# Token shifts behind the first inverse level, and level masks by group, in a one-core RWKV-7 / S5 / attention step

## The reference

```python
z_prev = jnp.concatenate([shift_prev[:, None], za[:, :-1]], axis=1)
zs = za + p['mu'] * (z_prev - za)          # the token shift ("mix")
...
def step(S, inp):                          # for each head, each token
    r_t, w_t, k_t, v_t, kk_t, b_t = inp
    sa = jnp.einsum('bhvk,bhk->bhv', S, -kk_t)
    S = S * w_t[:, :, None, :] + sa[..., None] * b_t[:, :, None, :] + v_t[..., None] * k_t[:, :, None, :]
    return S, jnp.einsum('bhvk,bhk->bhv', S, r_t)
```

## Time and profile before

| | |
|---|---|
| median of 3 runs | 1826.49 us (1825.55 to 1827.04) |
| the profiled execution | 1829.81 us, span 1828.1 us |
| TensorE matmul busy | 1654.1 us, 90% of the span |
| VectorE busy | 725.5 us, 40% |
| GpSimd busy | 601.0 us, 33% |
| ScalarE busy | 297.5 us, 16% |
| chain that ended last | TensorE 84%, VectorE 9%, GpSimd 3%, issue 2% |

### The profile page before, as it was taken

How to read it: one execution, slowest core, us unless ns; L and a number is a source line. 1 busy time by engine, 2 the same in 40 slices (tenths; PEclk the granted TensorE clock), 3 DMA queues, 4 the chain that set the end, 5 groups by cost and what they waited for, 6 DMA issues and landing times.

```text
span 1828.1 us, 33447 instructions
## 1 busy us (share of the span) xinstructions
PE 1654.1 (90%) x14584; PEld 1578.7 (86%) x14584; DVE 725.5 (40%) x1256; ACT 297.5 (16%) x483; POOL 601.0 (33%) x356
## 2 busy tenths in 40 slices
PE   5897776888887999999999999966899999999999
PEld 5896765776776999999999999954799999999999
DVE  5655766676664442200232112857243220022100
ACT  3001223221222211100121001133122110011100
POOL 3333234333202333334333333322133333334332
PEclk9998676889897999999999999966699999999999
DMA  7541001000003344444444444330044444444442
GB/s 289 143 163 37 7 13 28 2 15 15 2 15 123 115 141 159 148 151 138 146 156 157 139 138 142 135 115 1 1 142 148 148 138 140 159 161 138 145 160 98
DMA packets 41609, 201.58 MB, mean 110 GB/s; under 512 B 13888, under 2 KB 15040, under 8 KB 19008
## 3 DMA queue, kind: packets, MB, share of 16 engines
q1 hardware_dynamic: 19232, 96.89, 15.3%
q0 software_dynamic: 12528, 91.23, 14.9%
q10 hardware_dynamic: 9744, 11.88, 2.2%
HBM read 192.82 MB, written 6.37 MB: 109 GB/s over the span
## 4 chain that ended last, share of the span: by engine, by line
PE 84%; DVE 9%; POOL 3%; issue 2%; ACT 1%; DMA 1%; ACTq 0%; SPq 0%; DVEq 0%; POOLq 0%
PE PS L587 20%; PE PS L588 20%; PE PS L589 20%; PE PS L562 3%; PE PS L564 3%; PE PS L563 3%; PE PS L680 2%; PE PS L650 1%; PE PS L841 1%; PE PS L664 1%; PE PS L855 1%; PE PS L859 1%; PE PS L620 1%; POOL EE L518 1%; PE PS L611 1%
## 5 line engine op out<-in xcount | busy, mean ns | idle before, releaser
L412 POOL TENSOR_TENSOR WL<-WR,WH 128x2048 fp32r<-128x2048 f32 x87 | 406.7, 4675 | 457.4 <-DMA WH<-in_w 447.5
L587 PE MATMUL PS<-HH,WH 128*128 128x320 f32 x1344 | 417.3, 311 | 11.3 <-DVE Z L1587 9.6
L589 PE MATMUL PS<-HH,WL 128*128 128x320 f32 x1344 | 416.3, 310 | 0.0
L587 PE MATMUL PS<-XH,WH 128*128 128x320 f32 x1120 | 347.5, 310 | 0.4
L588 PE MATMUL PS<-XL,WH 128*128 128x320 f32 x1120 | 346.3, 309 | 0.0
L589 PE MATMUL PS<-XH,WL 128*128 128x320 f32 x1120 | 346.3, 309 | 0.0
L588 PE MATMUL PS<-HL,WH 128*128 128x320 f32 x896 | 277.0, 309 | 0.0
L587 PEld LDWEIGHTS PS<-HH,WH 128*128 128x128 f32 x1344 | 253.2, 188 | 13.1 <-DVE Z L1587 9.8
L589 PEld LDWEIGHTS PS<-HH,WL 128*128 128x128 f32 x1344 | 253.1, 188 | 0.0
L587 PEld LDWEIGHTS PS<-XH,WH 128*128 128x128 f32 x1120 | 210.3, 188 | 1.4 <-issue 1.1
L588 PEld LDWEIGHTS PS<-XL,WH 128*128 128x128 f32 x1120 | 210.3, 188 | 0.3
(11 more groups left out here) (389 smaller groups left out, 2298.6 us busy)
## 6 DMA issues: line engine op xcount, KB each, us to landing
WH<-in_w POOLq DMA_DIRECT2D x87, 1024.0 KB, 5.2
WR<-in_w SPq DMA_DIRECT2D x87, 1024.0 KB, 4.9
X<-in_xT SPq DMA_DIRECT2D x8, 320.0 KB, 11.0
out<-X ACTq DMA_DIRECT2D x8, 320.0 KB, 4.4
UR<-UF ACTq DMA_DIRECT2D x16, 80.0 KB, 4.3
UF<-UR SPq DMA_DIRECT2D x64, 20.0 KB, 1.8
WR<-in_wglu SPq DMA_DIRECT2D x1, 1024.0 KB, 5.0
S<-in_s ACTq DMA_DIRECT2D x4, 256.0 KB, 2.7
```

The source lines that it names most:

```text
L412: nc.gpsimd.tensor_tensor(WL[:, r], WR[:, r], WH[:, r].bitcast(F32), ALU.subtract).then_inc(w_split, 2)
L587: mm(out, wh[:, k, wc], xh[:, k, cols], start=(k == 0), stop=False)
L589: last = mm(out, wl[:, k, wc], xh[:, k, cols], start=False, stop=(k == kt - 1))
```

## The change

GpSimd waits for `tt_first` at 3p + 3 ahead of the token shifts of pair p + 1: they begin when VectorE has finished the third `tile_first` of pair p. And `tile_first` applies its two masks once to all tiles of a group, with the tile as one more dimension of the access patterns: in groups 0 and 1 two operations of 128 elements per partition become one of 256, both for L1956 and for L1958 (16 of each become 8 over the four pairs); group 2 keeps one of each.

```diff
@@ -476,6 +476,7 @@
                     pool.wait_ge(tr_done, 5 * p + 5)
                     if p + 1 < NPAIR:
                         pool.wait_ge(bonus_ready, p + 1)
+                        pool.wait_ge(tt_first, 3 * p + 3)
                         mix(4 + p + 1, RKV[:, 1]).then_inc(mixed, 1)
                         mix(p + 1, RKV[:, 0])
                         mix(8 + p + 1, RKV[:, 2]).then_inc(mixed, 1)
@@ -1952,11 +1953,11 @@
                 dve.wait_ge(lv_done, 3 * p + g + 1)
                 tv = TT[:, 512 * g:512 * g + 256 * n].rearrange("p (i a h k) -> p i a h k", a=2, h=2, k=64)
                 ba = GM[:, 1024 * g:1024 * g + 512 * n].rearrange("p (h i a k) -> p i h a k", h=2, a=4, k=64)
-                for i in range(n):
-                    tt(tv[:, i, 0], PS[:, BANK[g]:BANK[g] + 2, 64 * i:64 * i + 64],
-                       half_mask(C_L1).unsqueeze(1).broadcast_to((P, 2, 64)), M)
-                    last = tt(tv[:, i, 1], ba[:, i, :, 0], half_mask(C_U1).unsqueeze(1).broadcast_to((P, 2, 64)), M)
-                o(last)
+                every = (P, 2, n, 64)
+                ps = PS[:, BANK[g]:BANK[g] + 2, 0:64 * n].rearrange("p h (i k) -> p h i k", k=64)
+                tt(tv[:, :, 0].rearrange("p i h k -> p h i k"), ps, half_mask(C_L1).unsqueeze(1).unsqueeze(1).broadcast_to(every), M)
+                o(tt(tv[:, :, 1].rearrange("p i h k -> p h i k"), ba[:, :, :, 0].rearrange("p i h k -> p h i k"),
+                     half_mask(C_U1).unsqueeze(1).unsqueeze(1).broadcast_to(every), M))
                 tf = TT[:, 512 * g:512 * g + 256 * n].rearrange("p (a k) -> p a k", k=64)
                 tt(tf, tf, I64.unsqueeze(1).broadcast_to((P, 4 * n, 64)), A).then_inc(tt_first, 1)
```

## The result

The changed kernel takes **1840.22 us** (four runs, 1838.34 to 1843.73) against 1826.17 for the kernel before (four runs, 1825.55 to 1827.04): a ratio of 1.0071, with an interval of 1.0046 to 1.0097. Measured again beside other kernels it took 1837.91 us against 1830.30, a ratio of 1.0044 (1.0029 to 1.0060). It is slower, by 0.4 to 0.7%. The forecast was 1830.5 us with a range up to 1836: the sign was right, the size was not. In the three later sets of runs the kernel before took 1830.15, 1830.30 and 1829.93 us; the ratios given for these sets lie 0.01 to 0.26% above the plain quotients of the medians, most in the first set.

A forecast was written before the change was run, and what follows sets the result against it. Bound: a chain alternating between TensorE, VectorE and ScalarE, its VectorE part lengthened by GpSimd. Pairs 1, 2, 0 and 3 sum 1.7 + 1.4 + 0.9 - 0.05 = +4.0 us, giving 1830.5 us; range 1823.0 to 1836.0.

The forecast's parts named there:

- The masks: VectorE's masks: running without GpSimd saves 3.53 us in pairs 1 and 2; wider operations save 0.15 in pairs 0 to 2.
- The shifts become the late one: GpSimd's delayed shifts, not ScalarE, release `rates`: pair 1 at 398.6 us, where it could start at 395.2.
- The whole gain is lost in this wait: Before `rates` in pair 1: the 3.5 us gained ahead is used up waiting for shift V.
- `masked` beside `rates`: Behind shift V, two `masked` operations each go ahead of a `rates` operation: 2.0 us, bounds 0 and 2.0.
- The clock: TensorE's clock after over 4 us idle before its third level: taken as 0, range -3 to +6 over three pairs.
- a rival with a chance of 0.13: Idle time before the third level lowers TensorE's clock from there: +4 and 1.5 per pair, 1835 us; chance 0.13.
- Pair 3: Last head pair, without token shifts: only the wider masks help, -0.05 us.
- The signs: Profile after: undisturbed masks, shifts starting 5.2 us behind evacuation, L425 releasing `rates`, L1860 to L1862 slow, pairs 70 to 71 us.

The follow-up runs named there:

- with `masked` out of the way: Changed kernel with the two `masked` operations waiting for the addition that follows `rates`; 1831.42 us, ratio 1.0020 to the kernel before.
- the kernel with TensorE kept busy: Changed kernel with eleven added 128x320 constant matmuls between TensorE's second and third levels in pairs 0 to 2; 1833.00 us, ratio 1.0042 to the kernel before.
- K and R early: Changed kernel with shifts K and R made in the previous pair's tail, only V behind the wait, `masked` after the last transpose; 1815.34 us, again 1819.12 us.

## Why the prediction was right and wrong

**The masks.** Right: 3.53 us was foretold for the wait and 0.15 for the wider masks, and 3.75 came for both (8.77 to 5.02). The wider masks' own share is 0.22 us in pair 1 (5.24 to 5.02) rather than 0.15.

**The shifts become the late one.** Right in mechanism and nearly in size: V was forecast at 20.7 us behind the evacuation in pairs 1 and 2, and `rates` was released at 20.57; in pair 0 at 19.9, and came at 19.27, since the collisions with `decay_sums` added 1.9 us to GpSimd's 12.72 there and 2.4 in pair 1, where I had added 2.8. "The whole gain is lost in this wait" is what the chain of waits now shows, GpSimd's operations standing in it one after the other, to `rates` and TensorE's third level:

```profile
404.35 1.27 POOL RKV L424
405.62 0.40 POOL RKV L425
406.11 1.26 DVE TP L1861
407.39 1.21 DVE Z L1862
...
409.96 0.70 DVE TT L1980
410.70 2.40 PE PS L842 x40
413.10 2.22 PE PS L703 x10
```

**`masked` beside `rates`.** Right in kind, 0.6 us too large: 2.0 us taken, 3.85 - 2.44 = 1.4 measured, and with `masked` out of the way 2.43. The first `masked` had already begun when `rates` was released, and each `masked` held VectorE for 0.7 us, not for its full 1.0.

So up to the addition behind `rates` the sum was -0.3 us in pair 0, +1.2 in pair 1 and +0.9 in pair 2, +1.8 together, where the working had +0.9, +1.9 and +1.6, 4.4 together. With pair 3's 1.5 us taken off, these waits alone would have left the kernel where it was. That it came out slower, as forecast, is owed to the next term, which the forecast put at nothing: the sign was right in good part by luck.

**The clock. This is the term that failed.** The working says "I take 0 and keep both for the range: -3 to +6". In its place the profiles show 9.8 us: the rest of each pair, from that addition to the next third Gram evacuation, went from 39.8, 45.5 and 45.7 us to 44.1, 48.5 and 48.2. Of these 9.8 us, 5.2 lie between the addition and `kk_inverse`, where the forty matmuls and the narrow tens stand, and 4.6 behind `kk_inverse`. That most of it is the clock's is shown by the kernel with TensorE kept busy, in which the same stretches add up to 131.9 us (131.1 before). Pair 0 shows it in small: before, its third level stood behind 1.56 us of idle TensorE and took 1.51 us; after, it stands behind 4.35 us and takes 2.40. How much of the 9.8 us one profile can vouch for is another matter: with the masks alone the idle time ahead of the third level was 1.56 and 1.57 us, the low level still fell on narrow tens of pairs 0 and 1 (2.12, and 1.70 and 2.27 us), and the same stretches added up to 134.5 us. So some 3 us either way are within what the clock does by itself here.

The prediction had the mechanism as a rival with a chance of 0.13 and had the prices at hand: 2.29 us for ten narrow matmuls at the low level, about 1.2 at the full one (1.28 in the timelines), and the idle time of over 4 us, which came as worked out. It fell short in two places. It put the low level at 1 to 2 us per pair, where 3.3 came on average, as the low level lay on forty matmuls, two tens and the matmuls behind them, some 9 us. And it balanced that by a gain from the present low stretch going away, which didn't happen: the end of pair 1's second level was granted 0.50 in both kernels (398 to 401 us before, 402 to 405 after). Keeping TensorE busy took 8.7 of the 11.4 us of pairs 0 to 2 away in the profile, with the shifts left as they are.

**Pair 3** gained 1.5 us, not 0.05. But over the nine profiles in which its code is that of the changed kernel it took 53.7 to 55.4 us, and with the masks tile by tile 55.4 and 55.7. Some 0.2 us are the wider masks; the rest can't be told from scatter.

**The range** missed for one more reason: both medians of the first set lie 14 us apart while the pairs explain 10. The second set gives 7.6. Even so its 1837.91 us lies above 1836.0. The three runs of before, with a spread of 1.5 us, were too few to show the scatter of this kernel: in the 45 later runs it ranged from 1823.9 to 1835.6.

**The signs** named in advance all came but one: the masks, the start of the shifts (5.27 us behind the evacuation), the release of `rates` by L425 and its two slow operations. The pairs of 69 us, foretold at 70 to 71, became 72.9 and 72.7: there the clock stands.

The lock of the shared port that the Trainium skill describes (SBUF — State Buffer, Who interferes with whom) agrees with these traces in both directions. Beside GpSimd the two-input mask, the scan and the tensor_scalar took up to 1.22, 2.44 and 1.25 us, without it 0.28, 1.49 and 0.49. The evacuation from PSUM with one SBUF input took 0.94 us beside it and 0.95 without.

## What to carry to other kernels

Work moved behind a point to avoid a collision has a due time of its own: work out when its last consumer starts (in the new schedule, not in the present one), and count everything queued in front of it. Here one of the three moved pieces (R) wasn't needed by that consumer, and another (K) could have been made long before; with R behind `rates`, or both made early, the kernel was 0.5 to 0.8% faster than before, where moving all three cost 0.4 to 0.7%. And when a change makes TensorE wait some microseconds longer, price the work behind that wait at its low clock before calling the clock an unknown.

## What wasn't expected of the hardware

- The low level shows behind the idle time rather than in it. In the changed kernel 408 to 411 us, almost idle, shows 0.85 and the busy stretch right behind it 0.50, for 9 us. The idle time alone doesn't fix what follows: behind 1.56 us, ten narrow matmuls of pair 0 took 1.28 us in the kernel before and 2.12 with the masks alone.
- Ten matmuls of two columns cost 1.28 us at full clock and 2.29 at the low level, as much as a level of forty 64x64 ones (1.38 to 1.51 against 2.40), and all of it stands on the chain of waits.
- The stretch from 150 to 307 us, the S5 mixer, goes back and forth between the two levels (0.68 to 0.72 on average in seven of the profiles), and the first third Gram evacuation behind it moved by 9 us among eleven profiles with the same code ahead of it. Two sets of runs gave ratios of 1.0071 and 1.0044 for the same two kernels; the pairs in their profiles agreed to 0.3 us. Here the length of the changed part was the surer measure, though it scatters too where the clock changes within it (pairs 0 to 2 of K and R early: 188.3 and 187.3).
